# The delta rule's triangular inverse accumulated in PSUM and copied by ScalarE, with four modulation chunks moved to other places

## The reference

```python
# first block: the delta rule, per head (4) and chunk of 64 tokens (4)
a_strict = jnp.where(strict, einsum(k_beta, k) * l_mask, 0.0)
t_mat = a_strict + jnp.eye(CHUNK)
value = triangular_solve(t_mat, v_beta, lower=True, unit_diagonal=True)
k_cumdecay = triangular_solve(t_mat, k_beta * jnp.exp(decay)[..., None], ...)
def step(S, inp):                       # over the 4 chunks
    v_new = val - kc @ S
    o = qd @ S + att @ v_new
    S = S * cd + kt.T @ v_new
mixed = jnp.concatenate([o_att, o_dn], axis=-1) @ w_out
h = h + mixed
h = h + jnp.square(jax.nn.relu(rms_norm(h, g) @ w_ff1)) @ w_ff2
# second block
mod = jnp.dot(jax.nn.silu(c), w_ada) + b_ada      # [6144] = 12 chunks of 512
sh1, sc1, g1, sh2, sc2, g2 = jnp.split(mod, 6, axis=-1)
h = rmsnorm(x, norm_mix) * (1.0 + sc1) + sh1      # then w_in_2, retention, differential attention
x = x + g1 * (merged @ w_out)
h2 = rmsnorm(x, norm_ffn) * (1.0 + sc2) + sh2     # then 32 experts of width 512
x = x + g2 * hierarchical_moe(h2, ...)
```

## Time and profile before

| | |
|---|---|
| median of 3 runs | 1146.23 us (1145.27 to 1148.15) |
| the profiled execution, its own time | 1137.32 us |
| span in its profile | 1135.5 us |
| PE busy | 1106.6 us (97%) |
| DVE, ACT, POOL busy | 603.9, 501.5, 151.2 us |
| granted TensorE clock | 9 tenths or more in every slice |
| DMA busy over the span | some 75% of the queues' 16 engines; 0.97 in the last 435 us |

### The profile page before, as it was taken

The page is one execution under the profiler, slowest core; times in us unless marked ns, Lnnn a source line. Parts: engine busy times, 40 slices in busy tenths (PEclk is TensorE's granted clock), DMA queues, the critical chain, the costliest instruction groups (busy, mean ns, idle before and its releaser), DMA issues.

```text
span 1135.5 us, 18601 instructions
## 1 busy us (share of the span) xinstructions
PE 1106.6 (97%) x7625; PEld 843.2 (74%) x7625; DVE 603.9 (53%) x925; ACT 501.5 (44%) x827; POOL 151.2 (13%) x111
## 2 busy tenths in 40 slices
PE   8999799999999999999999999999999999999996
PEld 7987678999878888778888876666666666666663
DVE  5988676879956784785755652222222222222223
ACT  6665654654433746645556252222222222222223
POOL 1339960422000040400000000000000000000000
PEclk9999999999999999999999999999999999999999
DMA  9862825477486756644548579999999999999994
GB/s 314 280 215 77 297 93 201 161 263 257 183 306 204 243 176 223 211 162 154 174 157 329 209 288 423 421 426 423 423 425 420 425 422 421 425 424 421 426 421 175
DMA packets 82701, 332.05 MB, mean 292 GB/s; under 512 B 4555, under 2 KB 6926, under 8 KB 66110
## 3 DMA queue, kind: packets, MB, share of 16 engines
q1 hardware_dynamic: 81236, 328.43, 74.6%
q0 software_dynamic: 1088, 2.34, 1.0%
q10 hardware_dynamic: 298, 0.11, 0.1%
HBM read 329.83 MB, written 1.05 MB: 291 GB/s over the span
## 4 chain that ended last, share of the span: by engine, by line
PE 80%; DVE 8%; DMA 7%; issue 2%; ACT 2%; SPq 1%; DVEq 0%; ACTq 0%
PE bank L1113 18%; PE bank L451 12%; PE bank L453 12%; PE bank L452 12%; PE bank L1132 9%; PE bank L1103 5%; DMA ring<-in_w_exp_down 3%; DVE ring_r L1844 2%; DMA ring<-in_w_in 2%; DVE arena L1924 2%; PE bank L1160 1%; PE bank L1161 1%; DMA ring<-in_w_ff 1%; DMA ring<-in_w_ada 1%; PE bank L1120 1%
## 5 line engine op out<-in xcount | busy, mean ns | idle before, releaser
L1844 DVE TENSOR_TENSOR ring_r<-ring,arena_r 128x2048 fp32r<-128x2048 f32 x93 | 217.9, 2355 | 118.5 <-ACT arena_r L1333 116.9
L1333 ACT ACTIVATE arena_r<-ring 128x2048 fp32r<-128x2048 f32 x93 | 177.4, 1918 | 170.1 <-PE bank L453 71.7
L453 PE MATMUL bank<-arena_r,actT_r 128*128 128x512 f32 x384 | 150.5, 392 | 0.0
L451 PE MATMUL bank<-arena_r,tok_r 128*128 128x512 f32 x352 | 140.8, 400 | 1.7 <-DVE con L2331 1.7
L452 PE MATMUL bank<-ring_r,tok_r 128*128 128x512 f32 x352 | 138.2, 393 | 0.0
L2688 POOL TENSOR_TENSOR ring<-ring 128x512 f32<-128x512 f32 x63 | 102.5, 1652 | 253.7 <-ACT ring L1424 251.9
L2503 DVE TENSOR_TENSOR arena<-bank,arena 64x512 f32<-64x512 f32 x62 | 42.7, 688 | 175.3 <-PE bank L1132 174.6
L451 PE MATMUL bank<-tok_r,arena_r 128*128 128x256 f32 x352 | 99.5, 283 | 1.8 <-DVE actT_r L1861 1.2
L453 PE MATMUL bank<-tok_r,ring_r 128*128 128x256 f32 x352 | 98.3, 279 | 0.0
L452 PE MATMUL bank<-actT_r,arena_r 128*128 128x256 f32 x352 | 98.2, 279 | 0.0
L2489 DVE TENSOR_TENSOR arena<-bank,arena 128x256 f32<-128x256 f32 x32 | 13.6, 425 | 151.3 <-ACT arena L1763 93.9
(11 more groups left out here) (424 smaller groups left out, 1770.7 us busy)
## 6 DMA issues: line engine op xcount, KB each, us to landing
ring<-in_w_in SPq DMA_DIRECT2D x22, 2048.0 KB, 9.6
ring<-in_w_exp_down SPq DMA_DIRECT2D x22, 2048.0 KB, 21.3
ring<-in_w_exp_gate SPq DMA_DIRECT2D x21, 2048.0 KB, 21.9
arena<-in_w_exp_up SPq DMA_DIRECT2D x21, 2048.0 KB, 23.5
ring<-in_w_ff SPq DMA_DIRECT2D x16, 2048.0 KB, 7.8
ring<-in_w_ada SPq DMA_DIRECT2D x12, 2048.0 KB, 10.9
arena<-in_w_exp_gate SPq DMA_DIRECT2D x11, 2048.0 KB, 21.5
arena<-in_w_exp_down SPq DMA_DIRECT2D x10, 2048.0 KB, 21.4
```

Of the source, the lines that this page charges most:

```text
L451: mm(o, l[0], r[0], start=start, stop=False)
L453: return mm(o, l[1], r[0], start=False, stop=stop)
L1333: A(hi, w, ACT.Copy).then_inc(S["w_high"], 1)
L1844: TT(half(i, ringR)[0], w, hi.bitcast(fp32), ALU.subtract).then_inc(S["w_rest"], 1)
```

## The change

The inverse and its transpose now stay in one PSUM bank per tile (`held`): `D0` is multiplied into it, and each level's matmuls add to it there (`start=False`). ScalarE copies the bank to SBUF after each level (`inverse_copies`), where VectorE made two additions. The two held banks are left out of the turns. The gate's product is split into halves over levels 0 and 1, and no modulation chunk is turned within the levels. Chunks 1 and 0 are added up by GpSimd (0 also scaled by it), starting when the gate product has been read, and turned behind `kc` and behind the recurrence. Chunk 2 is summed whole by VectorE just ahead of `o_rest(1)` and turned after `out_product(1, 1)`. Chunk 3 takes the place of 5 in ff1, and chunks 4 and 5 come behind ("win2", 10) and ("wret", 0) in the ring, are summed by VectorE in steps 9 and 13 and turned after steps 11 and 14. Three of the eight heads' exponentials go behind the copies of `val` and `kc`, and one before them. VectorE's sum of chunk 8 moves from x=4 to x=3 in ff2.

```diff
-        ET, DI, DT, YY, AT, MT = [x[:, 0:8 * C] for x in (ar(15360, 1024), DQ, DK, QD, kbT, qT)]
+        ET, YY, AT, MT = [x[:, 0:8 * C] for x in (ar(15360, 1024), QD, kbT, qT)]
+        DIT = [x[:, 0:8 * C] for x in (DQ, DK)]
...
-        ADA_BY_POOL = (0, 4)
-        ADA_BY_DVE = (7, 8, 9)
-        DVE_MOD = {4: 8, 10: 9}
-        ADA_FF1 = {2: 5, 5: 6}
+        ADA_BY_POOL = (1, 0, 3, 6, 10, 11)
+        ADA_BY_DVE = (2, 7, 8, 9, 4, 5)
+        DVE_FF2 = {3: 8, 10: 9}
+        DVE_STEP = {9: 4, 13: 5}
+        ADA_FF1 = {2: 3, 5: 6}
...
-        ADA_STEP = {3: 10, 6: 11}
-        ADA_Z = {1: 5, 6: 6}
+        ADA_STEP = {3: 10, 6: 11, 11: 4, 14: 5}
+        ADA_Z = {1: 3, 6: 6}
...
-        ADA_BEHIND = {("win", 2): (0,), ("win", 6): (1, 2, 3, 4), ("ff1", 2): (5,), ("ff1", 5): (6,), ("ff2", 0): (7,),
-                      ("ff2", 3): (8,), ("ff2", 6): (9,), ("win2", 2): (10,), ("win2", 6): (11,)}
+        ADA_BEHIND = {("win", 6): (1, 0), ("wout", 1): (2,), ("ff1", 2): (3,), ("ff1", 5): (6,), ("ff2", 0): (7,),
+                      ("ff2", 3): (8,), ("ff2", 6): (9,), ("win2", 2): (10,), ("win2", 6): (11,), ("win2", 10): (4,),
+                      ("wret", 0): (5,)}
...
+        uses, where, base, turns, held = [0] * 8, {}, [0] * 8, [0], []
 
         def job(name):
+            while turns[0] % 8 in held:
+                turns[0] += 1
             turns[0] += 1
             return job_at(name, (turns[0] - 1) % 8)
...
-                    by_pool = [x for x in range(c + 1) if x not in ADA_BY_DVE]
-                    pe.wait_ge(S["pool_step"], 1 + 3 * len(by_pool) + sum(x <= c for x in ADA_BY_POOL))
+                    pe.wait_ge(S["pool_step"], 4 + 3 * ADA_BY_POOL.index(c) + (c != 1))
...
                     for r in (0, C):
-                        i = mm(bk[r:r + C, h * C:(h + 1) * C], within(DT)(4 * t + h, r), K("identC")[r:r + C, :],
-                               start=True, stop=True)
+                        mm(bk[r:r + C, h * C:(h + 1) * C], turned_inverse(4 * t + h, r), K("identC")[r:r + C, :],
+                           start=(h == 0), stop=True, skip_group_check=True)
+                for h in range(DH):
+                    for r in (0, C):
+                        i = mm(bk[r:r + C, (4 + h) * C:(5 + h) * C], K("identC")[r:r + C, :], turned_inverse(4 * t + h, r),
+                               start=False, stop=True, skip_group_check=True)
                 end(i, f"D0{t}")
+                held.append(where[f"D0{t}"][0])
...
+            def dg_half(h):
+                w = wait_split("win", 6, h)
...
             def fill(l):
-                if l == 0:
-                    split_product("win", 6, "dg")
-                elif l == 1:
-                    ada(0)
+                if l < 2:
+                    dg_half(l)
                 elif l == 2:
-                    ada(1)
                     att_turn()
                 elif l == 3:
                     att_scores((0, 1))
-                else:
-                    ada(2)
+                elif l == 4:
                     att_scores((2, 3))
 
             for l, s in enumerate(LEVELS):
                 last = s == LEVELS[-1]
                 for t in range(T):
-                    wait_read(pe, f"D0{t}" if l == 0 else f"Dn{l - 1}{t}")
-                    product(f"Y{l}", AT, DI, t)
+                    wait_read(pe, f"D{l}{t}")
+                    chunk_products(f"Y{l}", t, lambda bk, h, r: bk[r:r + C, h * C:(h + 1) * C], within(AT), inverse)
                     if t == 0:
                         fill(l)
                 for t in range(T):
                     wait_read(pe, f"Y{l}{t}")
-                    if l:
-                        wait_read(pe, f"Dt{l - 1}{t}")
-                    if not last:
-                        product(f"Dn{l}", DT, YY, t)
-                    product(f"Dt{l}", YY, DT, t)
+                    bk = begin_at(f"D{l + 1}{t}", held[t])
+                    for turned in (1,) if last else (0, 1):
+                        for h in range(DH):
+                            for r in (0, C):
+                                two = (turned_inverse(4 * t + h, r), within(YY)(4 * t + h, r))
+                                i = mm(bk[r:r + C, (4 * turned + h) * C:(4 * turned + h + 1) * C], two[turned],
+                                       two[1 - turned], start=False, stop=True, skip_group_check=True)
+                    end(i, f"D{l + 1}{t}")
+            held.clear()
...
-            ada(3)
+                        if h == DH - 1:
+                            end(i, f"kc{t}_{r}")
+            ada(1)
...
-            ada(4)
+            ada(0)
...
             out_product(1, 1, lambda: turn_x1(0))
+            ada(2)
...
+            ada_scaled(1)
             token_copies("av", av)
-            for t in range(T):
-                bk = wait_full(act, f"D0{t}")
-                done(copy(DI[:, t * 256:(t + 1) * 256], bk[:, 0:256]), f"D0{t}")
-            ada_scaled(1)
+
+            def inverse_copies(l, ts=range(T)):
+                for t in ts:
+                    bk = wait_full(act, f"D{l}{t}")
+                    o = slice(256 if l == len(LEVELS) else 0, 256 if l == 0 else 512)
+                    done(copy(DIT[t][:, o], bk[:, o]), f"D{l}{t}")
+
+            inverse_copies(0)
...
+            inverse_copies(1)
             for t in range(T):
...
             nc.scalar.preload_act_table_set("natural_log_exp_and_others")
-            ada_scaled(2)
+            inverse_copies(2)
...
-            ada_scaled(3)
...
-                    act.wait_ge(S["a_max"], h + 1)
-                    act.sem_inc(read[where[f"as{h}"][0]], 1)
+                    wait_read(act, f"as{h}")
...
-            att_exps(range(4))
-            att_exps(range(4, 8))
+            inverse_copies(3)
+            att_exps((0,))
+            inverse_copies(4)
+            att_exps((1, 2, 3))
+            inverse_copies(5)
+            att_exps((4,))
...
+                att_exps((5,) if t == 0 else (6, 7))
...
-            def corrected(l, t):
-                o = slice(t * 256, (t + 1) * 256)
-                if l < len(LEVELS) - 1:
-                    bk = wait_full(dve, f"Dn{l}{t}")
-                    done(TT(DI[:, o], bk[:, 0:256], DI[:, o], ALU.add), f"Dn{l}{t}")
-                bk = wait_full(dve, f"Dt{l}{t}")
-                done(TT(DT[:, o], bk[:, 0:256], DT[:, o], ALU.add), f"Dt{l}{t}")
...
-            for l in range(len(LEVELS)):
-                masked(l, 0)
-                if l == 0:
-                    dve.wait_ge(S["a_rs"], 1)
-                    for xt in range(3):
-                        head_scaled(xt)
...
-                elif l == 3:
-                    dve.wait_ge(S["bias_masked"], 1)
-                    biased_scores(range(4))
-                elif l == 4:
-                    biased_scores(range(4, 8))
-                    mod_cols(2)
-                masked(l, 1)
-                corrected(l, 0)
-                if l == 0:
...
+            masked(0, 0)
+            dve.wait_ge(S["a_rs"], 1)
+            head_scaled(0)
+            head_scaled(1)
+            masked(0, 1)
+            head_scaled(2)
+            head_scaled(3)
+            masked(1, 0)
+            tt(v3(KBE, 8), v3(KB, 8), bc(edec, P), ALU.mult)
+            masked(1, 1)
+            gated(0)
+            masked(2, 0)
+            gated(1)
+            for t in range(T):
+                bk = wait_full(dve, f"aT1{t}")
+                done(TS(v3(aqkT[1], 4)[:, :, t * P:(t + 1) * P], v3(bk[:, :], 4), col("kg"), None, ALU.mult), f"aT1{t}")
+            masked(2, 1)
+            masked(3, 0)
+            dve.wait_ge(S["bias_masked"], 1)
+            biased_scores((0, 1))
+            masked(3, 1)
+            biased_scores((2, 3))
+            masked(4, 0)
+            biased_scores((4, 5))
+            masked(4, 1)
+            biased_scores((6, 7))
...
-            mod_cols(3)
             new_state(0)
+            mod_cols(1)
...
             w_rest(F0 + 3)
+
+            def mod_sums(c):
+                n = place[("ada", c)]
+                dve.wait_ge(w_in[n % NR], 16 * (n // NR + 1))
+                w = weights("ada", c)
+                step(TS(w[:, 0, :], w[:, 0, :], cs[:, 0:1], None, ALU.mult))
+                for k in range(1, KT):
+                    i = STT(w[:, 0, :], w[:, k, :], cs[:, k:k + 1], w[:, 0, :], ALU.mult, ALU.add)
+                    if k < KT - 1:
+                        step(i)
+                i.then_inc(S["mod_summed"], 1)
+
+            mod_cols(0)
+            mod_sums(2)
             o_rest(1)
-            mod_cols(4)
-            for c in range(4):
-                wait_read(dve, f"mod{c}")
-            step(STT(sc1, modc[:, 8:16], 1.0, col("nmix", 0, 8), ALU.add, ALU.mult))
...
+            mod_cols(2)
...
-                if x in DVE_MOD:
-                    mod_sums(DVE_MOD[x])
+                if x in DVE_FF2:
+                    mod_sums(DVE_FF2[x])
+            for c in range(4):
```

(14 more changed lines are left out.)

74 lines of the change are left out of this document (31 added, 43 removed).

## The result

| | kernel before | changed kernel |
|---|---|---|
| all runs shown, median | 1146.12 us | 1137.66 us |
| lowest and highest | 1145.27, 1148.15 us | 1135.75, 1138.89 us |
| profiled execution | 1137.32 us, span 1135.5 | 1135.75 us, span 1133.6 |
| TensorE, VectorE, ScalarE busy | 1106.6, 603.9, 501.5 us | 1108.3, 605.8, 495.2 us |
| GpSimd busy | 151.2 us | 99.1 us |

The ratio of the times is 0.9922, with a 95% interval of 0.9902 to 0.9943: 8.5 us faster. The forecast was 2.6 us faster. Between the two *profiled* executions, though, the difference is only 1.6 us, 1.9 in the span. So there are two questions: whether the terms of the sum show in the trace, and where the other 7 us are.

The account below looks back on a forecast made before the run. TensorE, busy 97% of the span, bounds the kernel, so only its idle time or own work can give gains. Terms sum to -2.6 us, 1146.2 to 1143.6 us (0.23% less), range 1139.0 to 1148.0.

Parts of the forecast that it names:

- The levels, -7.1: D0 to the first `val` matmul: 34.8 us instead of 41.9, with 2.0 us of waits left; 7.1 us gained.
- Chunk 2, +4.1: Tile 1's output product: VectorE's sum of this modulation chunk ahead of `o_rest(1)` makes TensorE start later; 4.1 us lost.
- Chunk 8, -1.1: ff2: this modulation chunk's sum starts while VectorE waits for weights, so TensorE's wait goes; 1.1 us gained, bounds 0 and 1.1.
- Turning the chunks, +1.3: Three turns leave the levels and come back behind `out_product(1, 1)` and steps 11 and 14, 0.42 us each; 1.3 us lost.
- `mod_cols(2)`, +0.2: Ahead of ff1's second half: 0.9 us of VectorE work where it had about 1 us to spare; 0.2 us lost.
- The loads: ff1's weight loads are issued on later events; its second costs nothing if it lands within 14 us, median 7.8.
- The sum, -2.6: All terms added, -7.1 + 1.3 + 4.1 + 0.2 - 1.1, against the profiled execution: 1137.3 becomes 1134.7 us.
- I carry the difference: The profiled execution's 8.9 us below the runs' median is kept unchanged, so 1146.2 becomes 1143.6 us.
- The hidden sum: Rival, 15%: VectorE has more room ahead of `o_rest(1)`, so the 4.1 us loss there falls away; 1139.5 us.
- The levels kept no waits: Rival, 20%, claimed the opposite: half of the 6.1 us of old waits due to go there stay; 1146.6 us.
- ff1 didn't starve: Rival, 5%, claimed it would: weight loads landing in 23.5 us make TensorE wait 9 us in ff1; 1152.6 us.
- the second table load: Rival, 3%: ScalarE's table switch takes twice its row, so level 2's copy comes 1.28 us later; 1144.7 us.

Follow-up runs that it names:

- the levels alone: New delta levels and inverse copies, with the modulation where the kernel before has it, against the kernel before: median 1141.04 us, ratio 0.9961.

## Why the prediction was wrong

**The levels, -7.1.** Right in the profile, as a stretch: 34.8 us forecast, 34.8 measured, and both idle places near their sizes. What I took as one edit was two: the modulation's leaving carries 5.2 us, the inverse in PSUM 2.0 on top of it. The prediction's turned chunks are in the first of these, and so is the last mask, at 135.40 behind `mod_cols(2)` and at 130.24 without it. The 8.07 us of idle time there were the largest part of TensorE's idle time ahead of the experts (17.8 us up to 700 us), but not most of it.

**Chunk 2, +4.1.** The wait is there, 3.95 us. The term was mis-sized by what follows the pause: TensorE goes on at the lower clock. With transposes in it, the same wait leaves a kernel 1.8 us (profiled executions) to 3.8 us (medians) shorter. Taken away, with the small waits that come in its place, it gives 3.3 to 4.9 us, and with the sum behind the additions 6.0.

**Chunk 8, -1.1.** Measured 1.2, between two chips. **Turning the chunks, +1.3, and `mod_cols(2)`, +0.2** were not measured by themselves; in the profile no new wait stands at either place. **The loads:** there is no wait of TensorE for a weight load in ff1, as said.

**The sum, -2.6,** is near the difference of the two profiled executions, -1.6. The 1.0 us between them is less than the 1.8 us that the changed kernel loses at the lower clock behind its wait. The range has a slip: 1 us on either side of 1139.5 and 1146.6 is 1138.5 to 1147.6.

**The step that failed** is the one sentence "I carry the difference". I saw that the profiled execution of the kernel before lay 8.9 us below the median of its runs, and took these 8.9 us as a constant of the kernel. They are none. Two of three executions are 7 to 15 us longer than the median of the rest, at a lower mean clock. Where such executions were profiled, the clock falls at the idle end of the levels, and filling that idle time leaves no long execution. The one that was profiled ahead of the prediction is of the other kind. The change removes that wait, so it removes this too. Reckoned afterwards with this term, -2.6 - 8.8 (the medians of the long and the short runs) is -11.4 us against the median; the changed kernel gives 1.8 to 3.8 back to the clock at the output product: -7.6 to -9.6, and -8.5 was measured.

**The rivals.** None had this. The hidden sum had a time nearer by, 1139.5 us, but its mechanism didn't happen: the wait is there. The levels kept no waits but the two forecast, ff1 didn't starve, and the second table load took its row alone (112.04 for 1.28 us, the next copy at 113.33).

What stays open: why one execution in three of the kernel before is spared, why the fall comes right behind the wait in one long execution and mostly at 160 us in the other and lasts as it does, and why 4.85 us of idle time in the levels alone bring a short fall only. No run here shows it.

## What to carry to other kernels

When the profiled execution is shorter than the median of the runs, find out what the others contain before costing a change against it: here the wait worth most was the one whose idle time shows as 2.8 us in the good execution and costs 9 us more in the usual one. An idle TensorE can have a price beyond its length, and the length doesn't tell it: 2.8 us of it cost 9 us more here, 3.95 us cost 1.8 to 3.8, and behind 4.85 us the clock was back within 8. So look at the granted clock behind each long wait, in a usual execution, and try useless matmuls in it where it can't be removed (7 us here, at no cost in the chain, and a loss at the other two places). And when a copy is put into a chain of short steps, first take every long block (here 5 us of scaling) out of that engine's queue.
